# Six mixers without full stops: row tiles turned as they are stored, and odd attention's first scores inside the projection

## The reference, cut to what matters

```python
def first_block(x, mem, ...):                      # DEPTH = 2
    for layer in range(DEPTH):
        mix = even_mixer(x, ...) if layer % 2 == 0 else odd_mixer(x, ...)
        x = layer_norm(DEEPNORM_ALPHA * x + mix, ...)
        xa = memory_cross_attention(x, mem, ...)
        x = layer_norm(DEEPNORM_ALPHA * x + xa, ...)
        x = layer_norm(DEEPNORM_ALPHA * x + swiglu(x, ...), ...)

def memory_cross_attention(x, mem, wq, wkv, wo):   # 4 heads of 256
    q = (x @ wq).reshape(B_, S, X_HEADS, X_HEAD_DIM) * (X_HEAD_DIM ** -0.5)
    k, v = jnp.split(mem @ wkv, 2, axis=-1)
    p = jax.nn.softmax(jnp.einsum('bshd,bmhd->bhsm', q, k), axis=-1)
    return jnp.einsum('bhsm,bmhd->bshd', p, v).reshape(B_, S, D_MODEL) @ wo

def odd_mixer(x, w_in, lam_p, subln_g, w_out, lam_init):   # 8 heads, two score maps each
    q, k, v = jnp.split(x @ w_in, 3, axis=-1)
    q, k = rope(q), rope(k)
    o = diff_attention(q, k, v, lam)               # a = softmax(s0) - lam * softmax(s1); a @ v
    o = rms_norm(o, subln_g) * (1.0 - lam_init)
    return o.reshape(B_, S, C_WIDTH) @ w_out
```

## Time and profile before

| | |
|---|---|
| median of 3 runs | 3022.4 us (3019.59 to 3023.64) |
| profiled execution: time, span | 3025.01 us, 3023.2 us |
| mean granted TensorE clock | 0.989 |
| busy: PE, PEld, DVE, ACT, POOL | 2924.3, 2439.0, 921.0, 746.2, 1673.3 us |
| chain that ended last, by engine | PE 79%, DVE 8%, POOL 5%, DMA 4%, ACT 3% |
| HBM read | 266.79 MB, 89 GB/s over the span |

### The profile page before, as it was taken

How to read it: one execution, slowest core, us unless ns; L and a number is a source line. 1 busy time by engine, 2 the same in 40 slices (tenths; PEclk the granted TensorE clock), 3 DMA queues, 4 the chain that set the end, 5 groups by cost and what they waited for, 6 DMA issues and landing times.

```text
span 3023.2 us, 35556 instructions
## 1 busy us (share of the span) xinstructions
PE 2924.3 (97%) x14824; PEld 2439.0 (81%) x14824; DVE 921.0 (30%) x1424; ACT 746.2 (25%) x1492; POOL 1673.3 (55%) x1375
## 2 busy tenths in 40 slices
PE   8989999999999999999999999999999998999998
PEld 7877878888888668788888887788888887888887
DVE  3755204111025383032110234732110238521102
ACT  2236323101024373131010221542100133411001
POOL 5830571666656515716666567536666566066664
PEclk9999999999999999999999999999999998999999
DMA  4231331323223203313222233003322231033322
GB/s 146 93 136 43 126 112 55 99 98 98 98 92 111 70 15 114 124 42 112 98 98 98 84 105 98 15 29 112 98 98 98 92 104 62 29 112 98 98 98 84
DMA packets 184548, 271.21 MB, mean 90 GB/s; under 512 B 6708, under 2 KB 145972, under 8 KB 184388
## 3 DMA queue, kind: packets, MB, share of 16 engines
q1 hardware_dynamic: 174240, 243.28, 24.3%
q10 hardware_dynamic: 10148, 25.66, 2.5%
HBM read 266.79 MB, written 2.13 MB: 89 GB/s over the span
## 4 chain that ended last, share of the span: by engine, by line
PE 79%; DVE 8%; POOL 5%; DMA 4%; ACT 3%; issue 1%; ACTq 0%; DVEq 0%; POOLq 0%
PE PS L483 23%; PE PS L485 23%; PE PS L484 23%; POOL wlo L2358 4%; PE PS L847 3%; PE PS L833 2%; DVE a_qk L1268 1%; PE PS L570 1%; PE PS L994 1%; DMA raw<-mem_wkv 1%; ACT whi L610 1%; DVE nmx L1605 1%; PE PS L1455 1%; DMA raw<-ffn_w 0%; DVE s_c L2244 0%
## 5 line engine op out<-in xcount | busy, mean ns | idle before, releaser
L2358 POOL TENSOR_TENSOR wlo<-raw,whi 128x512 fp32r<-128x512 f32 x918 | 1200.4, 1340 | 550.8 <-ACT whi L610 550.8
L483 PE MATMUL PS<-xT_hi,whi 128*128 128x512 f32 (+1 forms) x2304 | 848.0, 368 | 18.7 <-POOL wlo L2358 10.0
L484 PE MATMUL PS<-xT_lo,whi 128*128 128x512 f32 (+1 forms) x2304 | 843.3, 366 | 0.0
L485 PE MATMUL PS<-xT_hi,wlo 128*128 128x512 f32 (+1 forms) x2304 | 843.1, 366 | 0.0
L2350 POOL TENSOR_SCALAR whi<-raw 128x1024 fp32r<-128x1024 f32 x384 | 416.6, 1103 | 656.1 <-DMA raw<-ffn_w 225.8
L483 PEld LDWEIGHTS PS<-xT_hi,whi 128*128 128x128 f32 x2304 | 435.6, 189 | 94.0 <-DVE xT_lo L590 8.6
L484 PEld LDWEIGHTS PS<-xT_lo,whi 128*128 128x128 f32 x2304 | 435.8, 189 | 70.4 <-issue 1.0
L485 PEld LDWEIGHTS PS<-xT_hi,wlo 128*128 128x128 f32 x2304 | 435.6, 189 | 70.3
L1037 DVE TENSOR_TENSOR htmp<-sil,PS 128x512 f32<-128x512 f32 x88 | 56.5, 684 | 804.4 <-ACT sil L1022 804.4
L483 PE MATMUL PS<-whi,h_hi 128*128 128x512 f32 x704 | 274.8, 390 | 1.5 <-POOL wlo L2358 1.5
L485 PE MATMUL PS<-whi,h_lo 128*128 128x512 f32 x704 | 274.0, 389 | 0.0
(11 more groups left out here) (384 smaller groups left out, 3117.3 us busy)
## 6 DMA issues: line engine op xcount, KB each, us to landing
raw<-ffn_w SPq DMA_DIRECT2D x66, 1024.0 KB, 5.0
raw<-ffn_w_gu SPq DMA_DIRECT2D x44, 1024.0 KB, 5.0
raw<-ffn_w_down SPq DMA_DIRECT2D x22, 1024.0 KB, 5.0
raw<-mem_wkv SPq DMA_DIRECT2D x16, 1024.0 KB, 5.2
raw<-even_w_in SPq DMA_DIRECT2D x14, 1024.0 KB, 5.2
raw<-ev_w_in SPq DMA_DIRECT2D x14, 1024.0 KB, 5.3
raw<-odd_w_in SPq DMA_DIRECT2D x12, 1024.0 KB, 5.1
raw<-od_w_in SPq DMA_DIRECT2D x10, 1024.0 KB, 5.2
```

The costliest lines, as they stand in the source:

```text
L483: pe.matmul(o, lhs[0], rhs[0], start=start, stop=False, skip_group_check=True)
L484: pe.matmul(o, lhs[0], rhs[1], start=False, stop=False, skip_group_check=True)
L485: return pe.matmul(o, lhs[1], rhs[0], start=False, stop=stop, skip_group_check=True)
L2358: m = pool.tensor_tensor(wlo[b][:, cs], raw[b][:, cs], whi[b][:, cs].bitcast(F32), ALU.subtract)
```

## The change

- The `phase_end` between units and rows goes from all six mixers, on all three engines; the one before the units goes from cross and odd. Those of even, hgrn and lru before their units stay.
- `pe_rows` waits, before tile t, for the store that completes row tile t (`o_out`).
- Cross: the first scores of each head wait for the evacuation of that head's queries.
- Odd: `first_scores` issues the scores of units 0 and 1 between the two halves of the last R job. ScalarE does the exponentials of these two units before it evacuates that job. The transposes of unit 0 wait for that evacuation (`free_banks`).
- Odd: VectorE's `dve_turn` of tile 0 comes before its last store.
- Odd: `d_p` and `d_a` move to the end of region W; `d_sq` and `d_pt` move over `d_cs` and `d_sw`.

```diff
@@ places of odd @@
         lam_tmp = d_tmp[:, 0, 0:128].rearrange("p (a d) -> p a d", a=2)
-        w = Area("X")
         d_p = w("d_p", [P, 3, 2, 512])
         d_a = w("d_a", [P, 3, 512])
+
+        w = Area("W", 4 * (8 * S + 8 * S + NT * D + NT * D))
+        d_sq = w("d_sq", [P, 2, 512])
         d_pt = w("d_pt", [P, 2, 512])
-        d_sq = w("d_sq", [P, 2, 512])
@@ pe_projections @@
                     for half in range(2):
                         (h, lo), = next_panel(pe)
+                        if half == 1 and between and j is jobs[-1]:
+                            between()
@@ pe_rows @@
-        def pe_rows(pe, row, k0, blocks):
+        def pe_rows(pe, row, blocks, stored):
+
             for t in range(NT):
+                pe.wait_ge(o_out, stored(t))
                 pe_turn(pe, row[:, t, :], blocks, 2 * t)
@@ act_units @@
-                if i < A.n:
+                if begun <= i < A.n:
                     exps(i)
@@ cross: act, dve, pe @@
                 evacuations(act, "act", q_jobs, evac)
-                phase_end(act, "act")
                 act_units(act, A, lambda u: softmax_exp(act, A, u, PS[:, A.ps(u), 0:MEM], 1.0, MEM, A.p(u)))
-                phase_end(act, "act")
                 act_rows(act, 0, KD)
...
                 pe_projections(pe, q_jobs)
-                phase_end(pe, "pe")
 
                 def scores(u, bank):
                     t, h = u // 4, u % 4
+                    if t == 0:
+
+                        pe.wait_ge(evac_act, q_jobs[h].done[1])
...
                 pe_units(pe, A, scores, values, lambda u: (exp_done, A.u0 + u + 1))
-                phase_end(pe, "pe")
-                pe_rows(pe, c_row, 0, KD)
+                pe_rows(pe, c_row, KD, lambda t: A.g0 + 2 * t + 2)
@@ even (hgrn and lru the same, with g_row, s_row; their waits for g_norm, lru_cut stay) @@
-                phase_end(pe, "pe")
-                pe_rows(pe, a_row, 0, KD)
+                pe_rows(pe, a_row, KD, lambda t: A.g0 + t + 1)
@@ odd: act @@
-                evacuations(act, "act", jobs, evac)
-                phase_end(act, "act")
+                evacuations(act, "act", jobs[:-1], evac)
...
-                act_units(act, A, exps, squares)
+                for u in range(2):
+                    exps(u)
+                evacuations(act, "act", jobs[-1:], evac)
+                act_units(act, A, exps, squares, begun=2)
                 squares(A.n + 1)
-                phase_end(act, "act")
                 load_next(act)
@@ odd: dve @@
                 evacuations(dve, "dve", jobs, evac)
-                phase_end(dve, "dve")
...
                 def store(g, bank):
                     rstd_ = rms_cols(g)[1]
+                    if g == A.groups - 1:
+
+                        dve_turn(dve, xT_hi, xT_lo, 0, KD, 0, 0, gain)
                     dve.wait_ge(rms_root, g + 1)
...
                 dve_units(dve, A, stat, store, mean_squares)
-                phase_end(dve, "dve")
-                for t in range(NT):
+                for t in range(1, NT):
                     dve_turn(dve, xT_hi, xT_lo, 0, KD, 2 * t, t, gain)
@@ odd: pe @@
                 pe_split(pe, jobs, 1)
-                pe_projections(pe, rest(jobs))
-                phase_end(pe, "pe")
...
-                pe_units(pe, A, scores, values, lambda u: (p_ready, u + 1))
-                phase_end(pe, "pe")
-                pe_rows(pe, d_row, 0, KD)
+
+                def first_scores():
+
+                    pe.wait_ge(evac_dve, rope_jobs[-1].done[1])
+                    pe.wait_ge(evac_act, jobs[-2].done[1])
+                    for u in range(2):
+                        for m in scores(u, A.ps(u)):
+                            m.then_inc(s_ready, 1)
+
+                def free_banks(u):
+                    if u == 0:
+                        pe.wait_ge(evac_act, jobs[-1].done[1])
+                pe_projections(pe, rest(jobs), between=first_scores)
+                pe_units(pe, A, scores, values, lambda u: (p_ready, u + 1), 2, free_banks)
+                pe_rows(pe, d_row, KD, lambda t: A.g0 + 2 * t + 2)
```

More of the change, by code:

```diff
@@ L485, in product, with pe_projections @@
             return pe.matmul(o, lhs[1], rhs[0], start=False, stop=stop, skip_group_check=True)
-        def pe_projections(pe, jobs, after=None, extra_job=None):
+        def pe_projections(pe, jobs, after=None, extra_job=None, between=None):
             free = {"act": evac_act, "dve": evac_dve, "gates": evac_gates}
@@ L849, in pe_units, with act_units @@
                     m.then_inc(pv_done, 1)
-        def act_units(act, A, exps, more=lambda u: None):
+        def act_units(act, A, exps, more=lambda u: None, begun=0):
             for i in range(A.n + A.lag):
@@ L2112, in pe @@
                 pe_units(pe, A, scores, values, lambda u: (exp_done, A.u0 + u + 1))
-                phase_end(pe, "pe")
                 pe.wait_ge(G["g_norm"], 3 * NT)
-                pe_rows(pe, g_row, 0, KD)
+                pe_rows(pe, g_row, KD, lambda t: A.g0 + t + 1)
             return {"act_load": act_load, "act": act, "dve": dve, "pe": pe, "pool": pool}
@@ L2302, in pe @@
                 pe_units(pe, A, scores, values, lambda u: (G["sb_weights"], u + 1))
-                phase_end(pe, "pe")
                 pe.wait_ge(G["lru_cut"], 8)
-                pe_rows(pe, s_row, 4, 4)
+                pe_rows(pe, s_row, 4, lambda t: A.g0 + t + 1)
             return {"act_load": act_load, "act": act, "dve": dve, "pe": pe, "pool": pool}
```

## The result

The kernel before took 3023.62 us (median of 5 runs, 3019.59 to 3036.72), the changed one 3004.12 us (5 runs, 3001.87 to 3006.29): a ratio of 0.9933 (95% interval 0.992 to 0.9945), and 19.5 us between the medians. Measured again later beside three other kernels: 3005.49 us (5 runs, 2998.96 to 3010.05), ratio 0.9935 (0.9922 to 0.9948). The forecast was 3005.4. The profiled execution took 3002.93 us (span 3001.1), 22.1 us less than that of before.

A forecast was written before the change was run, and what follows sets the result against it. TensorE, busy 97% of the span, was taken as the bound, so only its gaps could give time. Terms 4.1+1.6+3.0+2.3+6.0=17.0 us, off the median 3022.4, gave 3005.4; range 3002 to 3010, and 3000 to 3013 with rivals 1 and 2.

The forecast's parts named there:

- Four ends: Ends of cross (twice), hgrn and lru: row turns start without waiting for the last store; 4.1 us gained in sum.
- End of even: Even's end: earlier row turns and earlier load of `mem_row` start the output projection sooner; 1.6 us gained.
- End of odd: Odd's end: `mem_row`'s load, which ends last, is issued earlier; 3.0 us gained, bounds 1.3 to 3.0.
- some 0.7 late: Odd's end: VectorE's last store, behind tile 0's turn, ends at about 1125.3, some 0.7 us late.
- Start of cross: Both cross stages: the first score starts behind the projection's last product; 1.15 us gained each, 2.3 together.
- fixed distance: Start of cross: everything from first score to first exponential keeps its length, so the 1.15 us shift passes on whole.
- Opening of odd: Start of odd's units: two units' scores move into the last projection, hiding their statistics and exponentials; 6.0 us gained.
- combination 2 (half covered): Odd's opening: VectorE's combination 2 runs partly while POOL cuts a panel, ending 7.0 us after the projection's end.
- Rival 1: Odd's opening falls to 1.2 GHz again, keeping some 2 of the 6.0 us: 3009.4 us, chance 0.15.
- Rival 2: Even's and odd's ends: `mem_row`'s load lands no earlier, so 4.6 us of gain go: 3010.0 us, chance 0.07.
- Rival 3: Turns don't hold the clock up: every mixer's end falls to 1.2 GHz, 9.9 us lost: 3015.3 us, chance 0.03.
- Rival 4: The clock falls in odd's opening and stays down in its loop, 80 us lost: 3085 us, chance 0.03.

The follow-up runs named there:

- late cut: Changed kernel, but GpSimd cuts the third panel of odd's output matrix after odd's units, not under units 3 to 6: 3001.98 us; repeated, 3004.93 us.
- ends-only kernel: Changed kernel with the old starts of cross and odd, so only the six mixers' ends are changed: 3015.3 us; repeated, 3015.03 us.

## Why the prediction was right

**The sum.** 17.0 was forecast, the marks give 21.0 and the medians 19.5 and 19.0. The frame held: each stop gave time by its own marks, and no loss elsewhere stands out of the runs' spread. That the medians of 3004.12 and 3005.49 lie so near the forecast 3005.4 is partly luck. The terms came out 4.0 too small by the marks, the medians show 1.5 to 2 us less than the marks, and the kernel before measured 1.2 and 2.1 above the 3022.4 from which the sum was taken.

**Four ends** (1.09, 1.09, 1.06, 0.84). Mechanism right, size off by 0.33 to 0.36 each. The step that failed is "turn 0 starts at 473.77", right behind the last product's end. Turn 0 starts 0.16 before that end, as TensorE's instructions overlap when nothing is waited for, so its shift is 1.12 + 0.16 = 1.28 and not 1.09; another 0.13 is in the way from turn 0 to the output projection, 3.70 us instead of 3.83, where the wait of 0.15 for the low part is gone.

**End of even** (1.6, bounds 1.1 to 2.2). 1.76, and 2.6 against the second profile of before, in which the clock fell there. The load was issued under the last products, at 287.94, landed under turn 3, and never ended last.

**End of odd** (3.0). 4.23, past its upper bound, "by the load". Two steps failed. "ScalarE now issues it right behind its last squares": it is issued with their start, 0.6 us earlier. And "it lands at 1127.35 if it takes as long": it took 5.67 us before (5.3 in the second profile), at most 5.1 now. So the load lands just ahead, and what ends last is what the prediction had listed as "some 0.7 late": the last store behind tile 0's low part, on which turn 3 waits. Putting tile 0's turn behind that store gained nothing. The low clock of the lower bound came in one of the eight profiles that have this end as the change makes it (the late cut's first), and cost 1.36.

**Start of cross** (1.15 each). 1.63. That the first score "starts behind the projection's last product" was again too late by the overlap: the score's row starts at 439.81 under the last product's 439.58 + 0.39, which is 0.22 of the 0.48 missing. And the "fixed distance: the reduction, then ScalarE's load of the exponential's table" failed: the table load starts at 441.11, right behind the evacuation, 0.18 before the first statistic ends (440.87 + 0.42 = 441.29), where with the stop it had started 0.10 behind that end. So it is paid partly beside the reduction, which is the other 0.26. The two starts of cross were not divided by an experiment of their own.

**Opening of odd** (6.0, bounds 1 to 8.2). 6.3 against the first profile of before and 4.9 against the second, as the old opening held 10 and 7 us at the low clock. The steps end where they should, by a way that was partly another. From the last product's end (1024.54): statistic 3 ends after 4.6 us (predicted 4.8), statistic 5 after 10.5 (12.4), statistic 6 after 14.6 (14.8), statistic 7 starts after 15.7 (15.9), statistic 10 after 23.3 (23.5). The step "combination 2 (half covered)" failed: it was free, and combinations 3 and 4 took the stretch, 1.75 and 1.72 us against 0.75. The two accounts meet again at statistic 6. Cutting the panel later takes that away: 2.42 us, against the 2.2 between the estimate and its upper bound. The two parts of the edit were worth 3.85 for the stop alone (2.4 against the second profile of before) and 2.5 more net for the moved scores, by single profiles.

**Rival 1**, low clock in the opening: in none of the eight profiles with both parts of the edit at odd's opening (windows 1015 to 1060, clock 1.00); it came in the one without the moved scores. **Rival 2**, the load: counted from the last product it was issued 2.9 us earlier at even and 3.7 at odd, and where it is made late, these two ends lose 8 us. **Rival 3**: in the changed kernel's odd end the window from 1112 to 1115 holds turns and 1.76 us of idling at clock 1.00; in the late cut the same stretch fell to 0.55 in one execution and not in the other. And what the earlier trace rows shows of even's end in the kernel before, 1.00 throughout, did not repeat: behind the same 1.16 us of idling the clock fell under the row turns. The Trainium skill ("TensorE: Matmul & The Clock Gate", Part 4: PE-mode transpose) says that transposes do not count as activity like matmuls; as a rule that every mixer's end falls, the traces contradict it. But falls under turns are on record in one execution and not in the next, so the prediction's "the trace disagrees here" rested on one trace and said too much. **Rival 4**, a lasting low clock in odd's loop, came in none.

## What to carry to other kernels

A full stop between two phases costs little by itself (0.1 to 0.2 us of drain and handshake at four of the six ends here); what it costs is the filling that it forbids. So look for instructions of the next phase whose data has long been there, and for the load whose issue stands behind the stop. Price it from where an instruction starts that waits for nothing (here 0.16 us before the recorded end of the one ahead), and list what is late next: at odd's end, store, load and VectorE's low parts stood within a few tenths of each other. A single profile's total can be off by 10 us for reasons in code that was never touched. The marks around the edit repeat within 0.1 us where the clock does not fall between them; compare those, and take a second profile of the kernel before as well.

## What the runs showed of the hardware

- **The clock in even's attention.** Over a stretch in which TensorE is busy throughout by its records, whose ends are modelled (for example 20.00 of 20.00 us in the ends-only kernel, window 230 to 250, clock 0.50), the granted clock stayed low for 3.5 to 27 us from one execution to the next. What draws the length was not settled. Nor is idling alone a measure: after 2.19 us of it the clock stayed at 1.00 in one kernel, after 1.95 us it fell in another. Behind the same 1.16 us at even's end it fell in one execution of the kernel before and not in the other.
- **VectorE under GpSimd's cut.** The combination (L1598), which reads two operands from SBUF, took 1.72 to 1.75 us instead of 0.75 while GpSimd cut panels, and the small step ahead of it (L1593) 0.68 to 1.13 instead of 0.22; the maxima, which read PSUM, 1.21 us either way. With the cut behind the units the combination took 0.75 throughout. The Trainium skill ("SBUF — State Buffer", SBUF: two separate sides) says that the two engines exclude each other on a shared port pair when VectorE has two SBUF inputs and GpSimd's instruction reads SBUF; the traces agree.
- **ScalarE's table load** started 0.18 us before the statistic that its exponential waits for had ended, in all ten profiles without the stop in front of cross; in the four with it, 0.10 behind that end. What decides this was not looked into. **A DMA issue** on ScalarE's queue stood at the same 1109.65 as the start of the squares ahead of it.
